# The first mixer in another order, and norms whose sums are begun early

## The chip, the cores and the metric

One core of one Trainium2 chip runs the kernel. The metric is device time in microseconds of one execution, median over several. Five engines work in parallel and meet at semaphores: TensorE (PE; its weight loads are shown as PEld), VectorE (DVE), ScalarE (ACT), GpSimd (POOL), and SyncE (SP), which here only issues DMAs.

## The reference

Two stacks of two layers each follow one another on x of 256 tokens by 1024, all in float32. The change touches the input and mixer of the first layer and nearly all norms.

```
def hybrid_mixer(x, ...):                  # first layer
    xr, yr, q, k, v, iq, ik, iw = split(x @ w_in, [512, 512, 512, 64, 64, 256, 64, 4])
    xr = causal_depthwise_conv(xr, conv_w, conv_b)            # 4 taps
    rec = rg_lru(xr, ...) * gelu(yr)                          # linear recurrence over time
    att = dsa_attention(q, k, v, iq, ik, iw)                  # 8 heads of 64
    return concatenate([rec, att]) @ w_out
def rg_lru(x, ...):
    r, i = sigmoid(x @ w_a + b_a), sigmoid(x @ w_x + b_x)     # blocks of 64
    a = exp(-8 * r * softplus(-lam)); u = sqrt(1 - a * a) * (i * x)
    h[t] = a[t] * h[t-1] + u[t]
def dsa_attention(q, k, v, iq, ik, iw):
    isc = sum over h of relu(iq[h] @ ik) * iw[h]              # index scores, causal
    keep the 64 highest isc of each row; logits = q @ k * scale - slope * distance
    return softmax(logits over the kept ones) @ v
def first_block(x):
    for i in (0, 1):
        m = hybrid_mixer(x) if i == 0 else mla_mixer(x)
        h = layer_norm(ALPHA * x + m, ln1)
        f = square(relu(h @ w1)) @ w2; e = sigmoid(h @ w_gate) * (p @ w_proj)
        x = layer_norm(ALPHA * h + f + e, ln2)
def layer_norm(x): mu = mean(x); return (x - mu) * rsqrt(mean((x - mu)**2) + 1e-5) * g + b
def rms_norm(x):   return x * rsqrt(mean(x * x) + 1e-6) * g
```

The second stack has two layers, each with an RMS norm, dense projections with three token mixers (retention, a delta-rule recurrence, a short convolution), and 32 experts; a last RMS norm ends it.

## The kernel before

Features lie on the 128 partitions, tokens along the free dimension: a tile of xT, hT, R or SQ is 128 features by 256 tokens, eight of them make the width. A product "pair" is two output tiles of 256 tokens, each the sum of K products (8 for a width of 1024), in one of four PSUM banks; a product of float32 shows as two records. `bank_full` and `bank_read` count fills and evictions of each bank, which go round in the order of `BANK_USES`. Every engine has its instructions in an order written out by hand, and waits in it; SP issues weight blocks of 2 MB into the ring slots 0 to 3 as their last reader releases them.

First mixer. SP issues the constant table (4,179 columns, the identity first), the vectors, x, the gate blocks, two small column blocks for V, and w_in in blocks of 512 columns into slots 0 and 1. TensorE waits for constants and x, turns x into xT (L756), and runs eight pairs (`hy_in`: xr, yr, q, then K, index queries and index K; the 64 K columns and the 64 index-K columns stand twice in their block, put there by two DMAs each, so that both halves of the partitions get them). DVE and ACT evict them in turn. Then V with the index weights (`dsa_v`, 68 columns, 16 products), the index dots (`idx`), the gates (`rg_gates`, which wait for GpSimd's `conv_done`) and the attention. DVE makes the index scores (L1571, L1574), takes the top 64 by 8 rounds of MAX8 and MATCH_REPLACE8, and makes the mask (to L1593). GpSimd does the convolution (L2611 to L2616), the cubic part of gelu (L2624 to L2626), and parts of the decay (L2632 to L2637). In the attention, DVE's `masked_max` of a pair of heads (L1635 to L1647) and the four parts of the recurrence stand in one program: `recurrence(0)` is the reciprocal of L1603, parts 1 and 2 hold products and the scans (L1606 to L1618), part 3 the last product. GpSimd scales the probabilities (L2644), TensorE turns them (L823), ACT evicts (L2352), and TensorE makes the output. `hy_out` is four pairs, each evicted by DVE into R with ALPHA * x added (L1667).

Layer norm (`layer_norm` of each engine): TensorE sums the eight tiles of R over the partitions with a matrix of ones, so that each partition has the sum; DVE makes the mean (L1512) and takes it off R two tiles at a time (L1516); ACT squares (L2296); TensorE sums the squares; DVE makes variance plus epsilon (L1504), ACT the root (L2284), DVE the reciprocal (L1506) and scales tile by tile (L1520); ACT puts gain and bias on (L2289), and the next product starts on a tile when it is there (`ready`). `clear_acc` zeroes the accumulators of the feed-forward behind it. RMS norm: the same from the squares on, without a mean. Five RMS norms are here: two in the second layer's attention (of query and K/V), one ahead of each layer of the second stack, one at the end.

Of the kernel before, what the change touches and what calls it, by code (L numbers as in the profile page):

```python
# [19 lines left out]
P = 128  # L20
D = 1024
# [149 lines left out]
BANK_USES = [("x_in", 4), ("hy_in", 8), ("dsa_v", 1), ("idx", 4), ("rg_gates", 4), ("dsa", 4 * 2), ("hy_out", 4)]  # L171
# [96 lines left out]
def build(nc, a, out):  # L268

    with ExitStack() as ctx:  # L270
# [51 lines left out]
        def bcast(ap, n):  # L322
# [5 lines left out]
            "inputs_loaded", "x_loaded", "p_loaded", "small_loaded", "kvw_loaded", "tail_loaded", "pos_loaded",  # L328
            "lam_abs", "lam_log", "lam_ready", "conv_done", "decay_in", "decay_tanh", "decay_den", "decay_sqrt", "gelu_in", "gelu_sig", "rec_done",
            "dsa_max", "dsa_exp", "dsa_sum", "dsa_probs", "probs_turned", "probs_read", "att_full", "att_read",  # L330
            "norm_in", "norm_sum", "norm_centered", "norm_sq", "norm_var", "norm_std", "norm_scaled", "norm_out",
# [30 lines left out]
        VI = GT[:, 12:13, :]  # L362
        MIX = YB[:, 0:8, :]
# [6 lines left out]
        FF = PR[:, 32:40, :]  # L370

# [47 lines left out]
        def vi(tt, c0, c1):  # L419
            return flat(VI)[:, tt * 68 + c0:tt * 68 + c1]  # L420


        @block.sync
        def _(sp):
# [50 lines left out]
            def lin8(name, w):  # L475
# [3 lines left out]
            sp.dma_start(const[:], a["const"]).then_inc(sems["inputs_loaded"], 16)  # L479
            sp.dma_start(vec[:], a["vectors"]).then_inc(sems["inputs_loaded"], 16)  # L480
            sp.dma_start(R[:].rearrange("p (t k) s -> p t (k s)", t=TT), a["x"][0].rearrange("(t p) d -> p t d", p=P)).then_inc(sems["x_loaded"], 16)

            sp.dma_start(small_w[:], a["gate_blocks"]).then_inc(sems["small_loaded"], 16)
            w_in = a["hy_w_in"][0]
            tail = w_in[:, 1536:1988].rearrange("(k p) n -> p k n", p=P)
            sp.dma_start(GT[:, 20:24, :].rearrange("p a b -> p (a b)")[:, 0:KT * 68].rearrange("p (k n) -> p k n", k=KT)[:, :, 0:64],
                         tail[:, :, 64:128]).then_inc(sems["kvw_loaded"], 16)
            sp.dma_start(GT[:, 20:24, :].rearrange("p a b -> p (a b)")[:, 0:KT * 68].rearrange("p (k n) -> p k n", k=KT)[:, :, 64:68],
                         tail[:, :, 448:452]).then_inc(sems["kvw_loaded"], 16)


            s0, s1 = 0, 1
            r0 = ring[0][:].rearrange("p (k n) -> p k n", k=KT)
            r1 = ring[1][:].rearrange("p (k n) -> p k n", k=KT)
            sp.dma_start(r0, w_in[:, 0:512].rearrange("(k p) n -> p k n", p=P)).then_inc(slot_full[0], 16)
            sp.dma_start(r1, w_in[:, 512:1024].rearrange("(k p) n -> p k n", p=P)).then_inc(slot_full[1], 16)
            n0 = BANK_AT["hy_in"]
            sp.wait_ge(bank_full[(n0 + 1) % BANKS], filled(n0 + 1))
            sp.dma_start(r0, w_in[:, 1024:1536].rearrange("(k p) n -> p k n", p=P)).then_inc(slot_full[0], 16)
            sp.wait_ge(bank_full[(n0 + 3) % BANKS], filled(n0 + 3))  # L500
            for c, (c0, c1) in ((0, (0, 64)), (64, (0, 64)), (128, (128, 384)), (384, (384, 448)), (448, (384, 448))):

                sp.dma_start(r1[:, :, c:c + c1 - c0], tail[:, :, c0:c1]).then_inc(
                    slot_full[1] if c == 448 else sems["tail_loaded"], 16)
            released[0] = (bank_full[(n0 + 5) % BANKS], (n0 + 5) // BANKS + 1)
            released[1] = (bank_full[(n0 + 7) % BANKS], (n0 + 7) // BANKS + 1)
# [163 lines left out]
        def _(pe):  # L670
# [42 lines left out]
            def sums(src, K, piece, first=0):  # L713

                for i in range(K):
                    k = (first + i) % K
                    if k % 2 == 0:
                        piece(k // 2)
                    ins = mul(acc[3][:, 0:S], C("ones"), src[:, k, :], i == 0, i == K - 1)
                ins.then_inc(sems["norm_sum"], 1)  # L720

            def squared(q):
                pe.wait_ge(sems["norm_sq"], L.nxt("norm_sq"))

            def layer_norm(piece):
                sums(R, KT, piece)
                sums(SQ, KT, squared)
                L.nxt("norm_var")

            def rms_norm(src=SQ, K=KT, first=0):  # L730
                sums(src, K, squared, first)
                L.nxt("norm_var")
# [16 lines left out]
            pe.wait_ge(sems["inputs_loaded"], 32)  # L749
            pe.wait_ge(sems["x_loaded"], L.nxt("x_loaded", 16))  # L750
# [12 lines left out]
            n0 = BANK_AT["hy_in"]  # L763
            for b in range(4):
                pe.wait_ge(slot_full[b % 2], loaded(b // 2))
                if b == 3:
                    pe.wait_ge(sems["tail_loaded"], L.nxt("tail_loaded", 64))
                W = slot(b % 2, KT)
                for j in range(2):
                    pair(n0 + 2 * b + j, lambda h, k: W[:, k, (2 * j + h) * P:(2 * j + h + 1) * P],  # L770
                         lambda k: xT[:, k, :], KT)
# [4 lines left out]
            for tt in range(TT):  # L776
                for k in range(KT):
                    ins = mul(bk(n)[:, tt * 68:(tt + 1) * 68], xT[:, k, tt * P:(tt + 1) * P], kvw[:, k, :],
                              k == 0, k == KT - 1)
# [1929 lines left out]
```

## Time and profile before

| | |
|---|---|
| median of 3 runs (lowest, highest) | 2717.18 us (2714.19, 2719.2) |
| the profiled execution, its span | 2715.58 us, 2713.7 us |
| mean granted TensorE clock of that execution | 0.922 of full |
| TensorE busy | 2266.8 us (84%) |
| DVE, ACT, GpSimd busy | 681.5 us, 375.7 us, 60.6 us |
| moved by DMA | 655.01 MB, mean 241 GB/s |

The profiler takes one execution, with the start and length of each instruction and what released it. Times count from the start of the span. A timeline row merges neighbours of one kind: its second number is the time from the first start to the last end, the count stands at its end, and in brackets is the engine's idle time ahead with what ended it. The granted clock is 1.00 at 2.4 GHz and 0.50 at 1.2 GHz. A busy engine is not at its peak, and an idle one costs nothing unless it is waited for.

### The profile page before, as it was taken

The numbers are of one execution on the slowest core, as the hardware profiler recorded it, in microseconds if no ns is written. First come the engines' busy times: TensorE is split into PE (matmuls) and PEld (weight loads), VectorE is DVE, ScalarE is ACT, GpSimd is POOL, SyncE is SP. The second block draws the span as 40 slices with busy tenths as digits, with TensorE's granted clock in tenths as the row PEclk, the third lists the DMA queues.
The fourth block names the chain that finished last, engine by engine and source line by source line (L and its number), as shares of the span: only waits on it lengthen the run. The fifth ranks groups of instructions, "written<-read, shape, count | busy, mean of one in ns | idle before, by whom it ended". The sixth has DMA issues, their size and how long they took to land.

```text
span 2713.7 us, 28029 instructions
## 1 busy us (share of the span) xinstructions
PE 2266.8 (84%) x12294; PEld 1634.7 (60%) x12294; DVE 681.5 (25%) x1233; ACT 375.7 (14%) x730; POOL 60.6 (2%) x69
## 2 busy tenths in 40 slices
PE   7599999989999899999966656569999997666665
PEld 6478887668888688998622222238898873222222
DVE  0723212433220454432210000015343221000002
ACT  0310011141000321011100000013111110000001
POOL 3200000010000000000000000000000000000000
PEclk9789999999999899999998888889999998778777
DMA  6047642208762333124899999963322389999996
GB/s 225 27 176 312 271 185 95 97 1 325 271 267 81 102 109 127 63 94 180 349 409 409 409 409 409 409 245 127 124 78 94 125 346 409 409 409 409 409 409 248
DMA packets 202986, 655.01 MB, mean 241 GB/s; under 512 B 15736, under 2 KB 20600, under 8 KB 198392
## 3 DMA queue, kind: packets, MB, share of 16 engines
q1 hardware_dynamic: 202872, 653.32, 62.4%
q8 instruction: 92, 1.51, 0.2%
q14 instruction: 22, 0.18, 0.0%
HBM read 652.25 MB, written 1.05 MB: 241 GB/s over the span
## 4 chain that ended last, share of the span: by engine, by line
PE 64%; DMA 28%; DVE 4%; ACT 2%; issue 1%; SPq 0%; POOL 0%; DVEq 0%; ACTq 0%
PE bank L676 63%; DMA PRGT<-in_w_exp_gate 8%; DMA PRGT<-in_w_exp_up 7%; DMA ring<-in_w_exp_up 6%; DMA ring<-in_w_exp_gate 3%; DMA PRGT<-in_w_exp_down 3%; DMA ring<-in_w_exp_down 1%; DVE stat L1506 1%; PE bank L1056 0%; DMA ring<-in_hy_w_in 0%; DVE sm L1644 0%; POOL PRGT L2644 0%; ACT R L2561 0%; DVE PRGT L1587 0%; DVE R L1603 0%
## 5 line engine op out<-in xcount | busy, mean ns | idle before, releaser
L676 PE MATMUL bank<-hT,ring 128*128 128x256 f32 x3392 | 755.8, 383 | 10.1 <-ACT hT L2289 10.1
L676 PEld LDWEIGHTS bank<-hT,ring 128*128 128x128 f32 x3392 | 645.5, 192 | 105.2 <-issue 17.2
L676 PE MATMUL bank<-PRGT,ring 128*128 128x256 f32 (+4 forms) x1936 | 415.0, 377 | 3.3 <-ACT PRGT L2289 2.2
L676 PEld LDWEIGHTS bank<-PRGT,ring 128*128 128x128 f32 (+3 forms) x1936 | 353.0, 187 | 61.8 <-issue 5.5
L676 PE MATMUL bank<-PRGT,R 128*32 128x512 f32 x1120 | 170.4, 741 | 107.5 <-DMA PRGT<-in_w_exp_up 69.2
L676 PE MATMUL bank<-ring,R 128*32 128x512 f32 (+1 forms) x960 | 157.7, 769 | 111.5 <-DMA ring<-in_w_exp_up 56.7
L676 PEld LDWEIGHTS bank<-PRGT,R 128*32 128x32 f32 x1120 | 35.5, 123 | 233.0 <-DMA PRGT<-in_w_exp_up 110.6
L676 PE MATMUL bank<-PRGT,SQ 128*32 128x512 f32 (+1 forms) x768 | 110.9, 654 | 72.4 <-DMA PRGT<-in_w_exp_down 61.3
L676 PEld LDWEIGHTS bank<-ring,R 128*32 128x32 f32 (+1 forms) x960 | 34.9, 130 | 226.5 <-DMA ring<-in_w_exp_up 93.1
L1685 DVE SCALAR_TENSOR_TENSOR PRGT<-PRGT,sm 128x3072 f32<-128x3072 f32 x28 | 95.7, 3419 | 233.8 <-DMA PRGT<-in_w_ada 233.7
L676 PEld LDWEIGHTS bank<-PRGT,SQ 128*32 128x32 f32 (+1 forms) x768 | 34.7, 133 | 135.6 <-DMA PRGT<-in_w_exp_down 83.9
L676 PE MATMUL bank<-xT,ring 128*128 128x256 f32 (+1 forms) x368 | 84.2, 393 | 9.5 <-DMA ring<-in_hy_w_in 5.5
L676 PE MATMUL bank<-ring,SQ 128*32 128x512 f32 (+1 forms) x448 | 59.3, 612 | 30.8 <-DMA ring<-in_w_exp_down 22.5
L2228 DVE TENSOR_TENSOR SQ<-SQ,bank 128x512 f32<-128x512 f32 x16 | 11.0, 688 | 294.1 <-ACT SQ L2570 294.1
L676 PEld LDWEIGHTS bank<-xT,ring 128*128 128x128 f32 (+1 forms) x368 | 71.2, 195 | 22.4 <-issue 10.6
L2231 DVE TENSOR_TENSOR SQ<-SQ,bank 128x512 f32<-128x512 f32 x16 | 11.0, 688 | 275.9 <-PE bank L676 275.9
L676 PEld LDWEIGHTS bank<-SQ,hT 128*128 128x128 f32 x512 | 63.4, 205 | 18.2 <-issue 18.2
L2376 ACT ACTIVATE PRGT<-bank 128x512 f32<-128x512 f32 x32 | 19.1, 597 | 373.0 <-PE bank L676 373.0
L676 PE MATMUL bank<-PRGT 128*128 128x128 f32 (+4 forms) x400 | 52.3, 306 | 20.8 <-DVE PRGT L1635 15.5
L2240 DVE COPY R<-bank 128x512 f32<-128x512 f32 x16 | 11.1, 692 | 231.9 <-PE bank L676 231.9
L2561 ACT ACTIVATE R<-bank,sm 128x128 f32<-128x128 f32 x64 | 24.1, 457 | 318.7 <-PE bank L676 318.7
L2426 ACT ACTIVATE PRGT<-bank 128x512 f32<-128x512 f32 x42 | 25.1, 597 | 305.6 <-PE bank L676 305.6
(324 smaller groups left out, 1871.3 us busy)
## 6 DMA issues: line engine op xcount, KB each, us to landing
PRGT<-in_w_exp_down SPq DMA_DIRECT2D x40, 2048.0 KB, 24.0
PRGT<-in_w_exp_gate SPq DMA_DIRECT2D x36, 2048.0 KB, 23.8
PRGT<-in_w_exp_up SPq DMA_DIRECT2D x34, 2048.0 KB, 24.3
ring<-in_mlp_w SPq DMA_DIRECT2D x32, 2048.0 KB, 7.7
ring<-in_w_exp_up SPq DMA_DIRECT2D x30, 2048.0 KB, 24.2
ring<-in_w_exp_gate SPq DMA_DIRECT2D x28, 2048.0 KB, 24.1
PRGT<-in_w_ada SPq DMA_DIRECT2D x32, 1536.0 KB, 10.6
ring<-in_w_exp_down SPq DMA_DIRECT2D x24, 2048.0 KB, 23.9
```

The costliest lines, as they stand in the source:

```text
L676: return mm(o, lhsT=lhsT, rhs=rhs, start=first, stop=last, **kw)
L1506: v.reciprocal(stat[:, 1, :], stat[:, 1, :]).then_inc(sems["vec_chain"], 1)
L1685: v.scalar_tensor_tensor(total, ADA[h], sm[:, bass.ds(k, 1)], total, ALU.mult, ALU.add).then_inc(sems["ada_summed"], 1)
L2228: v.tensor_tensor(SG, SG, bank[0][:, :], ALU.mult).then_inc(sems["vec_chain"], 1)
L2231: v.tensor_tensor(SG, SG, bank[1][:, :], ALU.mult).then_inc(sems["gu_read"], 1)
L2240: v.tensor_copy(YE[:, 0:512], bank[2][:, :]).then_inc(sems["y_read_v"], 1)
L2376: f(tile_, bk(n)[:, :], ACT.Relu).then_inc(bank_read[n % BANKS], 1)
L2426: f(flat(PR[:, in_tiles(p), :]), acc[b][:, :], ACT.Copy).then_inc(dense_read[b], 1)
L2561: ins = f(XS[:, k * P:(k + 1) * P], bank[3][:, (k - 4) * P:(k - 3) * P], ACT.Identity, bias=sm[:, SPERM + k:SPERM + k + 1], scale=sm[:, GP ...
```

## The change

First mixer. Only the identity's columns go ahead of x. The block w_in[:, 1536:1988] (K, V, index queries, index K, index weights) is loaded first, whole, by one DMA; K and index K are doubled by TensorE, which multiplies the same 64 columns into both halves of the output. V's two column groups are separate products now. The order of products is K and index (`hy_kv`), V, index dots, xr, the first yr pair, gates, the second yr pair, q, attention. The convolution's taps are made by ACT, and GpSimd only adds them; ACT has the decay's scaling and its denominator, the tanh with a scale, and all evictions but one. `recurrence(0)` stands ahead of the first `masked_max`, and the other parts stay behind their pairs of heads.

Norms. The variance is made as the mean of squares minus the squared mean, so squares are taken of R itself. In layer norm 1 GpSimd adds the pairs 0, 1 and 2 of R and of the squares, while the output product runs, and TensorE sums only those two tiles and pair 3. In layer norm 2 TensorE sums R and squares alternately, all 16 tiles. DVE scales each tile by the reciprocal root and takes mean times reciprocal root off it one tile behind. RMS norms: ACT takes the root right from the sum, with scale and epsilon; the last three have GpSimd add three pairs of squares. `gains(0)` moves behind the second layer's attention.

```diff
-BANK_USES = [("x_in", 4), ("hy_in", 8), ("dsa_v", 1), ("idx", 4), ("rg_gates", 4), ("dsa", 4 * 2), ("hy_out", 4)]
+BANK_USES = [("x_in", 4), ("hy_kv", 2), ("dsa_v", 1), ("idx", 4), ("hy_xr", 2), ("hy_yr0", 1), ("rg_gates", 4),
+             ("hy_yr1", 1), ("hy_q", 2), ("dsa", 4 * 2), ("hy_out", 4)]
...
+            sp.dma_start(const[:, 0:P], a["const"][:, 0:P]).then_inc(sems["x_loaded"], 16)
+            sp.dma_start(R[:].rearrange("p (t k) s -> p t (k s)", t=TT), a["x"][0].rearrange("(t p) d -> p t d", p=P)).then_inc(sems["x_loaded"], 16)
+            sp.dma_start(*hy_block(0, 1536, 1988)).then_inc(slot_full[0], 16)
             sp.dma_start(vec[:], a["vectors"]).then_inc(sems["inputs_loaded"], 16)
+            sp.dma_start(const[:, P:], a["const"][:, P:]).then_inc(sems["inputs_loaded"], 16)
+            sp.dma_start(*hy_block(1, 0, 512)).then_inc(slot_full[1], 16)
             sp.dma_start(small_w[:], a["gate_blocks"]).then_inc(sems["small_loaded"], 16)
...
+            def norm_of_output(m):
+                sq = L.nxt("norm_sq", 4) - 4
+                pe.wait_ge(sems["presummed"], L.nxt("presummed"))
+                add_up(TOTAL, tiles_of(RSUM, 0), True, False)
+                add_up(TOTAL2, tiles_of(SQ, 0), True, False)
+                pe.wait_ge(bank_read[m % BANKS], filled(m))
+                add_up(TOTAL, tiles_of(R, 3), False, True).then_inc(sems["norm_sum"], 1)
+                pe.wait_ge(sems["norm_sq"], sq + 4)
+                add_up(TOTAL2, tiles_of(SQ, 3), False, True).then_inc(sems["norm_sum"], 1)
+                L.nxt("norm_var")
...
+            def rms_norm_presummed(first, last):
+                sq = L.nxt("norm_sq", 4) - 4
+                pe.wait_ge(sems["presummed"], L.nxt("presummed"))
+                add_up(TOTAL, tiles_of(SQ, first), True, False)
+                pe.wait_ge(sems["norm_sq"], sq + 4)
+                add_up(TOTAL, tiles_of(SQ, last), False, True).then_inc(sems["norm_sum"], 1)
...
+            for j, (c_twice, c_once) in enumerate(((0, 128), (384, 256))):
+                n = n0 + j
+                pe.wait_ge(bank_read[n % BANKS], emptied(n))
+                o = bk(n)
+                for k in range(KT):
+                    for half in (slice(0, 64), slice(64, 128)):
+                        mul(o[half, j * S:(j + 1) * S], W[:, k, c_twice:c_twice + 64], xT[:, k, :], k == 0, k == KT - 1)
+                for k in range(KT):
+                    ins = mul(o[:, (1 - j) * S:(2 - j) * S], W[:, k, c_once:c_once + P], xT[:, k, :], k == 0, k == KT - 1)
+                ins.then_inc(bank_full[n % BANKS], 1)
...
+            pe.wait_ge(slot_full[1], loaded(0))
+            for j in range(2):
+                hy_pair(BANK_AT["hy_xr"] + j, slot(1, KT), 2 * j)
+            pe.wait_ge(slot_full[0], loaded(1))
+            hy_pair(BANK_AT["hy_yr0"], slot(0, KT), 0)
             pe.wait_ge(sems["small_loaded"], L.nxt("small_loaded", 16))
             pe.wait_ge(sems["conv_done"], L.nxt("conv_done"))
...
+            hy_pair(BANK_AT["hy_yr1"], slot(0, KT), 2)
...
-                for q in range(4):
-                    r_ = R[:, 2 * q:2 * q + 2, :]
-                    v.tensor_tensor(r_, r_, bcast(stat[:, 0, :], 2), ALU.subtract).then_inc(sems["norm_centered"], 1)
...
+                v.tensor_scalar(var, var, 0.0, 1e-5, ALU.max, ALU.add).then_inc(sems["norm_var"], 1)
+                inverse()
+                v.tensor_tensor(mean, mean, var, ALU.mult).then_inc(sems["vec_chain"], 1)
+                c0 = L.nxt("norm_centered", KT) - KT
+                v.tensor_tensor(R[:, 0, :], R[:, 0, :], var, ALU.mult).then_inc(sems["norm_centered"], 1)
+                dve.wait_ge(sems["vec_chain"], L.up())
                 for k in range(KT):
+                    if k + 1 < KT:
+                        v.tensor_tensor(R[:, k + 1, :], R[:, k + 1, :], var, ALU.mult).then_inc(sems["norm_centered"], 1)
+                    dve.wait_ge(sems["norm_centered"], c0 + k + 1)
+                    v.tensor_tensor(R[:, k, :], R[:, k, :], mean, ALU.subtract).then_inc(sems["norm_scaled"], 1)
...
+                if slopes:
+                    recurrence(0)
                 masked_max(0)
...
+                    if slopes and hp:
                         recurrence(hp)
...
+                f(stat[:, 1, :], acc[3][:, 0:S], ACT.Sqrt, bias=C("eps"), scale=1.0 / width).then_inc(sems["norm_std"], 1)
...
+                for c in (2 * j, 2 * j + 1):
+                    f(PR[:, XC + c, :], PR[:, XR + c, :], ACT.Identity, bias=V_("conv_b")[:, c:c + 1], scale=V_("conv_w3")[:, c:c + 1])
+                    for i in range(3):
+                        sh = 3 - i
+                        ins = f(TAP[i][:, c, sh:S], PR[:, XR + c, 0:S - sh], ACT.Copy, scale=V_(f"conv_w{i}")[:, c:c + 1])
+                    ins.then_inc(sems["conv_taps"], 1)
...
+                pool.wait_ge(sems["conv_taps"], c + 1)
                 for i in (2, 1, 0):
                     sh = 3 - i
+                    ins = g.tensor_tensor(dst[:, sh:S], dst[:, sh:S], TAP[i][:, c, sh:S], ALU.add)
...
+            def presum(a_, b_, c_):
+                sq = L.nxt("norm_sq", 4) - 4
+                pool.wait_ge(sems["norm_sq"], sq + 2)
+                chained(nc.gpsimd.tensor_tensor(both(a_), both(a_), both(b_), ALU.add))
+                pool.wait_ge(sems["norm_sq"], sq + 3)
+                nc.gpsimd.tensor_tensor(both(a_), both(a_), both(c_), ALU.add).then_inc(sems["presummed"], 1)
```

## Rows read from the trace of the kernel before

**Rows 1.** Page, part 4: the chain that ended last, by engine.

```profile
PE 64%; DMA 28%; DVE 4%; ACT 2%; issue 1%; SPq 0%; POOL 0%; DVEq 0%; ACTq 0%
```

**Rows 2.** Timeline, start: start us, us, engine, line, operation, tiles, count.

```profile
12.51 3.65 PE L756 MATMUL bank<-const,R 128*128 128x128 f32 x16 [12.51 <-DMA R<-in_x]
...
21.65 57.93 PE L676 MATMUL bank<-xT,ring 128*128 128x256 f32 x256 [5.49 <-DMA ring<-in_hy_w_in]
```

**Rows 3.** Windows: busy of PE, PEld, DVE, ACT, POOL; PE clock, DMA share, GB/s.

```profile
8.00:10.00 2.00, 0.00 (x0) 0.00 (x0) 0.00 (x0) 0.00 (x0) 0.00 (x0) 1.00 1.00 404
24.00:26.00 2.00, 2.00 (x6) 1.61 (x5) 0.00 (x0) 0.00 (x0) 0.00 (x0) 0.50 0.91 335
```

**Rows 4.** Timeline of the first mixer, until its attention begins.

```profile
42.52 0.72 POOL L2616 TENSOR_TENSOR PRGT<-PRGT,R 128x254 f32<-128x254 f32 x1
...
79.41 3.68 PE L676 MATMUL bank<-PRGT,xT 128*128 128x68 f32 x32
...
83.03 1.68 PE L676 MATMUL bank<-PRGT 64*128 64x128 f32 x16
...
84.64 3.72 PE L676 MATMUL bank<-PRGT,small_w 128*128 128x256 f32 x16
...
85.76 0.29 DVE L1571 TENSOR_SCALAR PRGT<-PRGT,sm 128x128 f32<-128x128 f32 x1 [1.91 <-ACT PRGT L2316]
...
93.75 2.35 POOL L2635 TENSOR_TENSOR PRGT<-PRGT 128x1024 f32<-128x1024 f32 x1
...
105.38 0.55 DVE L1635 SCALAR_TENSOR_TENSOR PRGT<-const,bank 128x384 f32<-128x384 f32 x1
```

**Rows 5.** Timeline of the first attention and its output product.

```profile
112.69 6.52 DVE L1603 RECIPROCAL R<-R 128x1024 f32<-128x1024 f32 x1
...
112.85 1.61 POOL L2644 TENSOR_TENSOR PRGT<-PRGT,sm 128x256 f32<-128x256 f32 x2 [14.01 <-DVE sm L1652]
...
123.10 3.48 POOL L2644 TENSOR_TENSOR PRGT<-PRGT,sm 128x256 f32<-128x256 f32 x2 [8.64 <-DVE sm L1652]
...
142.82 27.89 PE L676 MATMUL bank<-PRGT,ring 128*128 128x256 f32 x128 [0.47 <-ACT PRGT L2356]
```

**Rows 6.** Timeline of the same; groups of TensorE by shape (busy us, mean ns).

```profile
117.58 1.43 PE L676 MATMUL bank<-SQ,PRGT 128*64 128x256 f32 x8
...
L676 PE MATMUL bank<-ring 128*64 128x64 f32 x64 | 2.4, 226 | 0.0
```

**Rows 7.** Timeline of layer norm 1, first layer.

```profile
170.99 3.62 PE L676 MATMUL bank<-R,const 128*128 128x256 f32 x16
...
176.62 5.41 PE L676 MATMUL bank<-SQ,const 128*128 128x256 f32 x16 [2.01 <-ACT SQ L2296]
...
183.04 1.75 DVE L1506 RECIPROCAL stat<-stat 128x256 f32<-128x256 f32 x1 [0.48 <-ACT stat L2284]
...
184.83 2.77 DVE L1520 TENSOR_TENSOR R<-R,stat 128x256 f32<-128x256 f32 x8
...
186.04 15.80 PE L676 MATMUL bank<-hT,ring 128*128 128x256 f32 x64 [0.38 <-ACT hT L2289]
```

**Rows 8.** Timeline of layer norm 2, first layer.

```profile
447.62 3.62 PE L676 MATMUL bank<-R,const 128*128 128x256 f32 x16
...
462.56 26.28 PE L676 MATMUL bank<-xT,ring 128*128 128x256 f32 x112 [4.01 <-ACT xT L2289]
```

**Rows 9.** Timeline of later norms: two in the middle, the last one.

```profile
909.89 1.75 DVE L1506 RECIPROCAL stat<-stat 128x256 f32<-128x256 f32 x1 [0.48 <-ACT stat L2284]
...
915.26 2.50 DVE L1820 TENSOR_TENSOR SQ<-xT 128x512 f32<-128x512 f32 x4
...
916.00 6.11 PE L676 MATMUL bank<-SQ,const 128*128 128x256 f32 x16 [7.13 <-DVE SQ L1820]
...
1806.69 6.21 PE L676 MATMUL bank<-SQ,const 128*128 128x256 f32 x16 [4.18 <-ACT SQ L2296]
...
2695.83 4.25 PE L676 MATMUL bank<-SQ,const 128*128 128x256 f32 x16 [1.76 <-ACT SQ L2296]
```

More of the change, by code:

```diff
@@ L485, in _ @@
[L485 to L489, printed above, removed]
@@ L500, in _ @@
[L500 to L506, printed above, removed]
+            n = BANK_AT["dsa_v"]
@@ L507, in _ @@
+            sp.wait_ge(bank_full[n % BANKS], filled(n))
+            sp.dma_start(*hy_block(0, 512, 1024)).then_inc(slot_full[0], 16)
+            n = BANK_AT["hy_xr"] + 1
+            sp.wait_ge(bank_full[n % BANKS], filled(n))
+            sp.dma_start(*hy_block(1, 1024, 1536)).then_inc(slot_full[1], 16)
+            for s, n in ((0, BANK_AT["hy_yr1"]), (1, BANK_AT["hy_q"] + 1)):
+                released[s] = (bank_full[n % BANKS], filled(n))
             lin8("hy_out", a["hy_w_out"][0])
@@ L730, in rms_norm, with add_up, tiles_of @@
-            def rms_norm(src=SQ, K=KT, first=0):
-                sums(src, K, squared, first)
-                L.nxt("norm_var")
+            def add_up(o, tiles, first, last):
+                for i, t in enumerate(tiles):
+                    ins = mul(o, C("ones"), t, first and i == 0, last and i == len(tiles) - 1, skip_group_check=True)
+                return ins
+            TOTAL, TOTAL2 = acc[3][:, 0:S], acc[2][:, 0:S]
+            def tiles_of(src, *pairs):
+                return [src[:, 2 * q + h, :] for q in pairs for h in range(2)]
@@ L780, in _ @@
+                    ins = mul(o[:, 64:68], xT[:, k, tt * P:(tt + 1) * P], W[:, k, 448:452], False, tt == TT - 1 and k == KT - 1,
+                              skip_group_check=True)
             ins.then_inc(bank_full[n % BANKS], 1)
-            for m in range(BANK_AT["hy_in"] + 4, BANK_AT["hy_in"] + 8):
+            for m in (n0, n0 + 1):
                 pe.wait_ge(bank_read[m % BANKS], filled(m))
@@ L803, in _ @@
                     ins.then_inc(bank_full[n % BANKS], 1)
+            hy_pair(BANK_AT["hy_yr1"], slot(0, KT), 2)
+            pe.wait_ge(slot_full[1], loaded(1))
+            for j in range(2):
+                hy_pair(BANK_AT["hy_q"] + j, slot(1, KT), 2 * j)
+            for m in (BANK_AT["hy_q"], BANK_AT["hy_q"] + 1):
+                pe.wait_ge(bank_read[m % BANKS], filled(m))
             def attention(name, pairs, done, q, k, v):
```

301 lines of the change are left out of this document (160 added, 141 removed).

## The prediction

> **What bounds the kernel now.** I read the page's chain first: TensorE holds 64% of it and DMA 28% [rows 1]. The DMA part lies in the expert stages, whose loads are released by semaphores of the stage before, so whatever is saved ahead of them moves them whole. The change touches no expert stage; I therefore read only the first mixer and the nine normalisations, in the timeline, and ask at each place what ends the wait.
>
> First mixer. TensorE waits for x until 12.51 us, transposes it, and waits again, for the first weights, until 21.65 [rows 2]. It then runs 256 records of products, the V product, the index dots and the gates back to back until about 88.4 [rows 2, 4]. But the attention starts only at 105.38: DVE gets its first index score at 85.76 and needs 19.6 us for scores, top-64 and mask [rows 4]. That is the first exposed piece. The second lies in the attention: DVE works without a gap, and in it stands a 6.52 us reciprocal of the recurrence [rows 5]. The output product begins at 142.82.
>
> Normalisations. Layer norm 1 sums R on TensorE (3.62 us), lets DVE subtract the mean, squares, sums again (5.41 us, with a gap of 2 us ahead), then goes through variance, square root and reciprocal; TensorE gets its first tile at 186.04, 15.05 us after the first sum began [rows 7]. Layer norm 2 takes 14.94 [rows 8].
>
> **The change, part by part.** All times below are of the profiled execution (2715.58 us; its span is 2713.7). The median of the runs shown is 2717.18, 1.6 higher, and the forecast is carried over to it at the end.
>
> *Start.* x now queues behind 64 KB of the identity instead of the whole constant table and the vectors (2,089.5 and 201 KB). 2.28 MB at the 404 GB/s of [rows 3] is 5.6 us, so x lands at 12.4 - 5.6 = 6.8 (TensorE starts on it at 12.51 now). Transposes 6.9 to 10.5, last copy 11.2. The first weight block (8 x 128 rows of 452 columns, 1.85 MB) follows directly: 4.6 us, 11.4. Products start at 11.4 instead of 21.65. If the two interleaved neighbours (vectors, rest of the table) slow it, 13 to 15.
>
> *TensorE's work until the attention.* Before: 57.93 + 3.68 + 1.68 + 3.72 [rows 2, 4]. The 57.93 contain a beginning at the lower of the two clock levels (0.50, 1.2 GHz [rows 3]): at the rate of the output product, 27.89 for 128 [rows 5], 256 records are 55.8, so 2.1 were lost. The pause ahead shrinks from 5.5 us to about 1; I take half the loss, 57.0. The K and index-K columns, which were doubled by five small DMAs, are now doubled on TensorE: 16 more products of 64 columns. Do the halves run side by side? The row for 64-column products that alternate between halves says yes: 64 records in 2.4 us, 38 ns each, against the 115 ns of the V product's 68-column records with all 128 columns of weights [rows 4, 6]. The attention's output product says rather no: 1.43 us for 8 records of 768 streamed columns in two passes, which at 27.89/128 per 256 is 1.31 without any overlap [rows 6]; but there each half issues two in a row. I take overlap, 0 us; the other end is 16 x 2 x 0.218 = 7.0. The Trainium skill (TensorEngine Tiling (Array Packing), Key Properties) says that different tiles can load weights and multiply in parallel; by it the sum stands as it is, by the second row it would be 7.0 longer; this trace has a row on either side. The V product becomes 64 records (64 columns, then 4) instead of 32. At 68 columns one took 3.68/32 = 0.115 us, twice what its columns stream in, so I take it as the price of its weights and not of its columns: 64 x 0.115 = 7.4, +3.7; if the 4-column ones went by their columns, about +0.2. Sum: 57.0 + 7.4 + 1.7 + 3.7 = 69.8.
>
> *The gates' wait.* TensorE now stands in order at conv_done between hy_yr0 and the gates, with hy_yr1 and hy_q behind it. The last two taps come from ACT about 4 us after hy_xr's second pair; GpSimd needs 3 additions each, 0.72 [rows 4] + 0.1, so 2.5 us for a channel tile and conv_done is some 7.3 after that pair; hy_yr0 covers 7.0. Stall 0.5. If each addition costs what a GpSimd row costs beside DVE work with two inputs (3.48 against 1.61 [rows 5]), 12 additions take 19.9 and the stall is 8.
>
> *Index chain.* It starts at 11.4 + 1.2 + 13.9 + 7.4 + 1.7 + 1 = 36.6 and ends near 56.5, when TensorE has over 25 us of products left: hidden entirely. Without that cover it would cost its 19.6. Later slot loads are released 7 us or more before they are needed, as now. Next late is TensorE itself: 11.4 + 69.8 + 0.5 = 81.7, then 1.2 for the eviction of hy_q and the first logits. Attention at 82.9 instead of 105.38: **-22.5**.
>
> *Attention.* The gates are done near 61 and their denominator on ACT near 65, so the reciprocal runs at 65 to 72 under the products. DVE's sequence loses 6.52 [rows 5]: **-6.5**. The other parts stay where they were.
>
> *Layer norm 1, twice.* GpSimd adds the first three pairs (R and squares) during the output product, whose pairs are 6.9 us apart; a 512-wide addition is about 1.3 (between 0.72 for 254 and 2.35 for 1024 [rows 4]). TensorE then needs 8 products, 3.62: from 170.99 to 174.61, instead of two sums to 182.03. To the reciprocal it was 1.01 (183.04 - 182.03); one DVE operation more, 0.35 (2.77/8): 175.97; reciprocal 1.75: 177.72 [rows 7]. From its end to TensorE's first tile it was 1.25; mean times rstd, the next scaling and the subtraction stand ahead of it now, 3 x 0.35: 180.0. So 6.0 less each, **-12.0**. The tiles now come every 0.70 instead of 0.35 on DVE; while the clock is low a product takes 0.87 and this costs nothing; at the full clock up to 8 x 0.27 = 2 each.
>
> *Layer norm 2, first layer.* Squares are ready early, so 16 products run through from 447.62: 7.1 instead of about the 11.0 of layer norm 1; + 0.35 + 1.05: **-2.5** [rows 7, 8].
>
> *RMS norms.* ACT takes the root straight from the sum: half of that 1.01, **-0.5**, at the query norm (the K/V one is covered). In the second norm chain of the last first-block layer, layer norm 2 gains 3.5 at its reciprocal, but DVE's 17 operations of 0.35 push its squares to 6.4 us after it instead of 3.6 (915.26 - 911.64) and GpSimd's two additions (2.6) follow; then 4 products instead of 8, which ran mostly at the low clock (6.11 [rows 9]): 3.5 + 2.6 + 0.5 - 2.8 - 2.8 = **-1.0**; if GpSimd waits for DVE's squares, +1. Between the layers (6.21 for 8 products after the last square but one [rows 9]) half the products go, less the wait for an addition: **-2.1**. At the end the sums were paced by the squares and closed 1.2 after the last (4.25 [rows 9]); now GpSimd's second addition ends 0.6 after it and 4 products at the low clock take 3.5: +2.4 - 0.5 = **+1.9**, +0.4 at the full clock. The moved gains() runs under the 28 us of mla_out, where DVE waits.
>
> Sum: -22.5 - 6.5 - 12.0 - 2.5 - 0.5 - 1.0 - 2.1 + 1.9 = **-45.2**; 2670.4 in a profiled execution, 2672 as a median.
>
> **Rivals.**
> *A. GpSimd holds TensorE.* The convolution's additions and the early sums meet DVE's two-input operations. For: 3.48 against 1.61. Against: during the index chain DVE mostly runs one-input operations, and the 1024-wide GpSimd product there took 2.35 [rows 4]. +8 at the gates, +2 at the norms: 2682. Beside it the Trainium skill (SBUF — State Buffer, SBUF: two separate sides) calls the port that DVE and GpSimd share an exclusive lock for the whole instruction; by this rule only operations with two SBUF inputs or a two-port mode block, and the pair 3.48 and 1.61 agrees, the latter beside a reciprocal.
> *B. The halves take turns,* +7.0: 2679.
> *C. The tiles' pace decides in the norms.* At the full clock 2 each in four norms: +8 at most, 2676 to 2680.
> *D. No change:* the expert stages are DMA-bound and could absorb the gain, if their loads were not released by it. Against: TensorE waits for loads issued after merged and chunk_used. 2717.
> *E. Slower.* TensorE stays at the 1.2 GHz level through the mixer. Its 69 us of products would take 67 more: 2672 + 67 = 2739; it turns slower once 45 us of full-rate work run at half. Against: 57.93 for 256 records, with 55.8 at the full rate, leaves room for no more than the first few at half.
>
> **How the numbers follow.** Forecast 60%, A 12%, B 8%, C 12%, D 3%, E 2%, and 3% for a larger gain (start or clock better by over 7). The forecast's own range: start -1 to +3, clock 1.2 either way, gates 0 to 3, norms -2 to +3: 2666 to 2678. With A, B and C up to 2683; low end 2664. 0.2% is 5.4 us, about what a measurement of this kernel tells from no change. Faster 0.95, same 0.03, slower 0.02.
>
> **What would show it.** In the profile after: products starting near 11.4; the index score near 37 and its mask near 57 under running products; an idle stretch of TensorE at the gates (under 1 us right, 5 or more A); the two hy_kv banks taking about 14 us together (21 if B holds); attention at 83; output product at 113.8; first tile 9.0 us after layer norm 1's first sum. The forecast is wrong if the attention starts after 90, or if a norm gains under 4 us.

## The result, and the profile after

| | before | after |
|---|---|---|
| median (lowest, highest), same chip | 2716.03 us (2714.19, 2719.2), 4 runs | 2680.69 us (2677.28, 2684.91), 4 runs |
| ratio, 95% interval | | 0.9869 (0.9852 to 0.9887) |
| profiled execution, span | 2715.58 us, 2713.7 us | 2679.7 us, 2677.9 us |

The kernel is 35.3 us faster; the forecast was 45.2 us less. The spans differ by 35.8, so 9.4 of the predicted us are missing. I cut the span at seven starts that both traces show, into eight pieces. Each runs from one start to the next.

| until | before | after | change | predicted |
|---|---|---|---|---|
| first masked maximum | 105.38 | 87.21 | -18.2 | -22.5 |
| output product of the mixer | 37.44 | 31.08 | -6.4 | -6.5 |
| first tile behind layer norm 1 | 43.22 | 38.99 | -4.2 | -6.0 |
| first tile behind layer norm 2 | 276.52 | 275.01 | -1.5 | -2.5 |
| first tile behind the second layer norm 1 | 173.80 | 166.74 | -7.1 | -6.5 |
| first tile of the dense stage | 289.75 | 290.19 | +0.4 | -1.0 |
| last product of the last expert stage | 1764.27 | 1762.52 | -1.8 | -2.1 |
| end | 23.32 | 26.16 | +2.8 | +1.9 |

The chain that ended last, by engine, in the page after; it answers to [rows 1]:

```profile
PE 64%; DMA 29%; DVE 3%; ACT 1%; SPq 1%; POOL 1%; issue 1%; POOLq 0%; DVEq 0%; ACTq 0%
```

TensorE's timeline of the kernel after, from the first products to the output product (start us, us, engine, line, operation, tiles, count):

```profile
11.37 14.58 PE L671 MATMUL bank<-xT,ring 128*64 128x256 f32 x96 [1.65 <-DMA ring<-in_hy_w_in]
25.78 10.03 PE L671 MATMUL bank<-ring,xT 128*128 128x64 f32 x64
35.74 3.09 PE L671 MATMUL bank<-PRGT 64*128 64x128 f32 x16
38.77 21.58 PE L671 MATMUL bank<-xT,ring 128*128 128x256 f32 x96
61.06 3.69 PE L671 MATMUL bank<-PRGT,small_w 128*128 128x256 f32 x16 [0.72 <-issue]
64.59 20.88 PE L671 MATMUL bank<-xT,ring 128*128 128x256 f32 x96
86.21 2.53 PE L671 MATMUL bank<-PRGT 64*128 64x128 f32 x20 [0.73 <-issue]
...
118.29 29.66 PE L671 MATMUL bank<-PRGT,ring 128*128 128x256 f32 x128 [0.47 <-ACT PRGT L2435]
```

And DVE's beside it: the first index score, the end of the mask, the reciprocal of the recurrence, the first masked maximum.

```profile
39.71 0.29 DVE L1612 TENSOR_SCALAR PRGT<-PRGT,sm 128x128 f32<-128x128 f32 x1 [2.75 <-ACT PRGT L2367]
...
59.62 0.76 DVE L1634 TENSOR_SCALAR PRGT<-PRGT 128x384 f32<-128x384 f32 x1
...
68.41 6.55 DVE L1653 RECIPROCAL R<-R 128x1024 f32<-128x1024 f32 x1 [7.16 <-ACT R L2405]
...
87.21 0.55 DVE L1686 SCALAR_TENSOR_TENSOR PRGT<-const,bank 128x384 f32<-128x384 f32 x1 [12.25 <-PE bank L671]
```

Products start at 11.37 (before 21.65 [rows 2]; forecast 11.4). Index chain and reciprocal both end under running products, and DVE then waits 12.25 us for TensorE: the exposed 19.6 us of [rows 4] are gone. TensorE's two short waits are marked "issue", but the rows of the engines that it waits for by the program end 0.10 us before it starts: GpSimd's last additions of the convolution at 59.25 + 1.71 = 60.96, ahead of the gates at 61.06, and ScalarE's eviction of q at 86.11, ahead of the logits at 86.21.

```profile
59.25 1.71 POOL L2690 TENSOR_TENSOR PRGT<-PRGT,SQ 128x254 f32<-128x254 f32 x2
...
85.51 0.60 ACT L2333 ACTIVATE PRGT<-bank 128x512 f32<-128x512 f32 x1 [6.31 <-PE bank L671]
```

From xr's first product to the first masked maximum it is 87.21 - 38.77 = 48.44 us, where the forecast had 57.0 - 13.9 + 3.7 + 0.5 + 1.2 = 48.5. What is off stands before it: V and the index dots hold TensorE for 38.77 - 25.78 = 12.99 us where the sum had 7.4 + 1.7 = 9.1. The windows of that stretch say why (busy of PE, PEld, DVE, ACT, GpSimd; granted clock; DMA share; GB/s):

```profile
27.00:29.00 2.00, 2.00 (x21) 2.00 (x19) 0.00 (x0) 0.00 (x0) 0.00 (x0) 1.00 0.00 0
29.00:31.00 2.00, 2.00 (x14) 2.00 (x14) 0.00 (x0) 0.00 (x0) 0.00 (x0) 0.69 0.00 0
31.00:33.00 2.00, 2.00 (x12) 2.00 (x11) 0.00 (x0) 0.00 (x0) 0.00 (x0) 0.50 0.00 0
...
37.00:39.00 2.00, 2.00 (x11) 1.26 (x10) 0.00 (x0) 1.17 (x3) 0.00 (x0) 0.50 0.91 233
39.00:41.00 2.00, 2.00 (x8) 1.69 (x9) 1.18 (x4) 0.58 (x2) 0.00 (x0) 0.75 1.05 410
41.00:43.00 2.00, 2.00 (x11) 1.77 (x10) 1.86 (x5) 0.00 (x0) 0.00 (x0) 1.00 1.02 383
```

TensorE is shown busy without a gap here, and yet the granted clock falls to 0.50 (1.2 GHz) from about 30 to 40: 21 records in 2 us become 12. The same level stands at the output product's start (0.50 in 118 to 120, 0.52 in 120 to 122, then 1.00), which takes 29.66 us instead of the 27.89 of [rows 5].

Layer norm 1 of the kernel after: the sums, the reciprocal, the first tile.

```profile
148.23 1.03 PE L671 MATMUL bank<-PRGT,const 128*128 128x256 f32 x4
...
149.10 1.03 PE L671 MATMUL bank<-SQ,const 128*128 128x256 f32 x4
...
153.28 1.75 DVE L1549 RECIPROCAL stat<-stat 128x256 f32<-128x256 f32 x1 [0.48 <-ACT stat L2359]
...
157.28 1.19 PE L671 MATMUL bank<-hT,ring 128*128 128x256 f32 x2 [1.80 <-ACT hT L2340]
```

From first sum to first tile it is 9.05 us, 6.00 less than the 15.05 of [rows 7], as forecast. The two rows of four records each (two products) are the sums over the pair of tiles into which GpSimd has added three pairs, of R and of the squares. The next rows are of the three RMS norms that GpSimd serves in the kernel after (ahead of the dense stage, between the layers, the last): DVE's squares, GpSimd's additions, TensorE's sums; they answer to [rows 9].

```profile
876.83 2.49 DVE L1873 TENSOR_TENSOR SQ<-xT 128x512 f32<-128x512 f32 x4
878.20 2.25 POOL L2738 TENSOR_TENSOR SQ<-SQ 128x512 f32<-128x512 f32 x1 [292.03 <-DVE SQ L1873]
880.52 1.26 POOL L2740 TENSOR_TENSOR SQ<-SQ 128x512 f32<-128x512 f32 x1
881.84 3.78 PE L671 MATMUL bank<-SQ,const 128*128 128x256 f32 x8 [13.84 <-POOL SQ L2740]
...
1767.86 1.27 POOL L2738 TENSOR_TENSOR SQ<-SQ 128x512 f32<-128x512 f32 x1 [812.01 <-ACT SQ L2353]
...
2655.47 4.12 DVE L2312 SCALAR_TENSOR_TENSOR xT<-bank,mod,xT 128x256 f32<-128x256 f32 x8 [3.83 <-PE bank L671]
...
2658.26 1.27 POOL L2738 TENSOR_TENSOR SQ<-SQ 128x512 f32<-128x512 f32 x1 [811.99 <-ACT SQ L2353]
...
2659.60 1.26 POOL L2740 TENSOR_TENSOR SQ<-SQ 128x512 f32<-128x512 f32 x1
...
2660.92 3.78 PE L671 MATMUL bank<-SQ,const 128*128 128x256 f32 x8 [5.49 <-POOL SQ L2740]
...
2665.31 1.75 DVE L1549 RECIPROCAL stat<-stat 128x256 f32<-128x256 f32 x1 [5.72 <-ACT stat L2345]
```

The same 512-wide addition takes 2.25 us where DVE's squares run beside it, with both inputs in SBUF. It takes 1.27 beside L2312 of DVE, which reads one of its two tensors from a PSUM bank (2658.26; L2312 runs to 2659.59), and 1.26 with DVE idle (2659.60). At the end TensorE waits for the second addition, then sums in 3.78 us, where before the sums ran along with the squares [rows 9].

### The profile page after: what moved, and what is told of

It reads as the page before. It is cut to its first block, busy times and chain, and to the rows that moved or that the text cites. A ratio compares the mean times of both kernels' runs of the same rounds, so it can differ in the third digit from the quotient of the medians.

```text
span 2677.9 us, 28088 instructions
## 1 busy us (share of the span) xinstructions
PE 2240.8 (84%) x12302; PEld 1620.2 (61%) x12302; DVE 685.2 (26%) x1253; ACT 390.5 (15%) x754; POOL 59.7 (2%) x62
## 4 chain that ended last, share of the span: by engine, by line
PE 64%; DMA 29%; DVE 3%; ACT 1%; SPq 1%; POOL 1%; issue 1%; POOLq 0%; DVEq 0%; ACTq 0%
PE bank L671 64%; DMA PRGT<-in_w_exp_gate 7%; DMA ring<-in_w_exp_up 7%; DMA PRGT<-in_w_exp_up 5%; DMA PRGT<-in_w_exp_down 4%; DMA ring<-in_w_exp_gate 3%; DMA ring<-in_w_exp_down 2%; SPq L617 1%; DVE stat L1549 1%; PE bank L1101 1%; DMA ring<-in_hy_w_in 0%; DVE sm L1695 0%; POOL PRGT L2713 0%; PE bank L867 0%; ACT R L2641 0%
## 5 line engine op out<-in xcount | busy, mean ns | idle before, releaser
L671 PE MATMUL bank<-hT,ring 128*128 128x256 f32 x3392 | 757.3, 383 | 11.4 <-ACT hT L2340 11.4
L671 PE MATMUL bank<-xT,ring 128*128 128x256 f32 (+2 forms) x400 | 83.4, 388 | 7.0 <-ACT xT L2340 5.3
L671 PEld LDWEIGHTS bank<-xT,ring 128*128 128x128 f32 (+2 forms) x400 | 68.7, 183 | 21.5 <-issue 9.7
L671 PE MATMUL bank<-SQ,hT 128*128 128x128 f32 x512 | 65.0, 288 | 0.0
```

Of the source, the lines that this page charges most:

```text
L671: return mm(o, lhsT=lhsT, rhs=rhs, start=first, stop=last, **kw)
```

## The experiments

Each edit is against the kernel after. A kernel with one execution has its profile alone; the others have a median and a ratio to the kernel before, taken on the same chip.

| kernel | us | ratio (95%) |
|---|---|---|
| wide V products | 2673.69, one | |
| V and index weights in one product | 2670.67, 4 runs (2669.62 to 2674.84) | 0.9842 (0.9826 to 0.9859) |
| K halves one after the other | 2682.39, one | |
| last sum without GpSimd | 2674.55, one | |
| mixer's part alone | 2692.50, 4 runs (2689.36 to 2697.61) | 0.9914 (0.9897 to 0.9930) |
| norms' part alone | 2707.14, 7 runs (2702.56 to 2708.68) | 0.9967 (0.9956 to 0.9978) |
| squares on ScalarE | 2683.12, one | |
| recurrence back inside | 2686.21, one | |
| V in one + last sum without GpSimd | 2669.04, 5 runs (2667.18 to 2673.09) | 0.9835 (0.9822 to 0.9849) |
| the same + squares on ScalarE | 2669.82, 5 runs (2669.51 to 2674.98) | 0.9838 (0.9825 to 0.9852) |

**Does the shape of the V products bring the clock down?** The 4-column product of all k but the last gets 64 columns, of which 60 are read by nobody; the count of records stays.

```diff
+                    if k < KT - 1:
+                        mul(o[:, 64:128], xT[:, k, tt * P:(tt + 1) * P], ring[0][:, k * 452 + 448:k * 452 + 512], False, False,
+                            skip_group_check=True)
+                        continue
                     ins = mul(o[:, 64:68], xT[:, k, tt * P:(tt + 1) * P], W[:, k, 448:452], False, tt == TT - 1 and k == KT - 1,
```

> The changed kernel, but 14 of the 16 four-column products behind V stream 64 columns (the four and sixty of the neighbouring weights, whose sums nobody reads). Number of records stays 64. Theory (the V stage lost because its records carry so few columns that the granted clock fell to half, which then also slowed the index dots and the start of the xr products): V takes about 7.4 us instead of 10.0, the dots 1.7 to 2.2 instead of 3.0, the clock stays at 1.00, the attention starts about 4.5 us earlier than 87.2. Rival (the number of records alone sets the 10.0 us, or the clock would have fallen there anyway): V stays at 10.0 or grows, no change of the attention's start.

TensorE's timeline, and two windows over the stretch:

```profile
25.89 7.21 PE L671 MATMUL bank<-ring,xT 128*128 128x64 f32 x64
33.02 1.68 PE L671 MATMUL bank<-PRGT 64*128 64x128 f32 x16
```

```profile
25.00:29.00 4.00, 4.00 (x34) 3.87 (x32) 0.00 (x0) 0.60 (x1) 0.00 (x0) 1.00 0.00 0
29.00:33.00 4.00, 4.00 (x38) 4.00 (x36) 0.00 (x0) 0.00 (x0) 0.00 (x0) 1.00 0.00 0
```

The short products have sixteen times the columns, the records are as many, and the stage is 2.8 us shorter: the clock stays at 1.00. V and index dots take 34.64 - 25.89 = 8.75 us, against the forecast's 9.1, and the first masked maximum comes at 82.49, 4.7 us earlier (the theory had 4.5). So the forecast's price of a record was right (7.21/64 = 0.113 us at the full level); what it lacked was the clock.

**One product instead of two.** Both column groups lie 384 apart, and one product takes 64 columns of each (128 streamed, 68 used).

```diff
+                    if k < KT - 1:
+                        w_ = ring[0][:, k * 452 + 64:k * 452 + 832].rearrange("p (b c) -> p b c", b=2)[:, :, 0:64]
+                        mul(two(o), x_, w_, tt == 0 and k == 0, False, skip_group_check=True)
+                        continue
```

> The changed kernel with V and index weights as one product of 128 columns in two blocks (68 of them used) for 7 of 8 pieces, so 36 records instead of 64. Theory (64 records at the price of their weights, and the clock lost besides): V takes 4.2 us, the dots 1.7 to 2.0, the attention starts 7 to 8 us earlier than 87.2; the time falls by 7 to 8, to about 2673, a ratio to the kernel before of 0.984. Rival (only the number of records counts, without the clock): 4.4 earlier, about 2676. Rival 2 (TensorE's end is not what starts the attention): no change.

The masked maximum starts at 79.33, 7.9 us earlier than in the kernel after, as the theory had it. The median is 10.0 us lower; by the ratios, each to the kernel before run beside it, it is 7.3. The V row:

```profile
25.84 4.08 PE L671 MATMUL bank<-ring,xT 128*128 128x128 f32 x36
```

36 records in 4.08 us are again 0.113 each, and 28 of them stream 128 columns: up to 128 the columns cost nothing here.

**Do the halves of K run side by side?** The loops over k and over the halves change places.

```diff
-                for k in range(KT):
-                    for half in (slice(0, 64), slice(64, 128)):
+                for half in (slice(0, 64), slice(64, 128)):
+                    for k in range(KT):
```

> The changed kernel, but the doubled K and index-K products run all eight pieces of one half and then all eight of the other, instead of alternating. Theory (two 64-column products run side by side only if neighbours in the queue go to different halves): each of the two doubled blocks takes 6.9 us instead of 3.6, so hy_kv takes 21 us instead of 14.4, and the attention starts about 6.6 later. Rival (64-column products cost half as much for another reason, fewer weights to load): no change.

```profile
11.20 21.80 PE L671 MATMUL bank<-xT,ring 128*64 128x256 f32 x96 [1.37 <-DMA ring<-in_hy_w_in]
```

21.80 us instead of 14.58, both at clock 1.00. The 7.2 us are the 7.0 that my sum gave for no overlap. So both rows of [rows 6] are right: neighbours in different halves overlap, two in a row in one half do not. The masked maximum starts at 92.68, 5.5 later; in this execution the V stage gave 2.1 back (7.95 us for 10.03), since the clock fell later in it.

**The last norm's sum in the old way,** from four pairs of squares, each as it comes.

```diff
-            rms_norm_presummed(3, 2)
+            for q in (3, 0, 1, 2):
+                pe.wait_ge(sems["norm_sq"], L.nxt("norm_sq"))
+                ins = add_up(TOTAL, tiles_of(SQ, q), q == 3, q == 2)
+            ins.then_inc(sems["norm_sum"], 1)
...
-            presum(3, 0, 1)
```

> The changed kernel, but the last norm sums its squares on TensorE pair by pair as they come (8 products), without GpSimd. Theory (the sums were paced by the squares before, and GpSimd's chain ends later than they did): from the last expert product's end of accumulation to the end 22.9 us, which is 0.5 less than before and 3.3 less than the 26.2 of the changed kernel. Rival (the longer end comes from the clock or the output's DMA): it stays at 26.

Rows of this kernel:

```profile
2649.72 3.69 PE L671 MATMUL bank<-stat,R 128*128 128x256 f32 x16 [0.86 <-DVE R L2297]
...
2655.17 4.24 PE L671 MATMUL bank<-SQ,const 128*128 128x256 f32 x16 [1.76 <-ACT SQ L2356]
...
2660.11 1.75 DVE L1552 RECIPROCAL stat<-stat 128x256 f32<-128x256 f32 x1 [2.55 <-ACT stat L2348]
```

From the last product to the end it is 2672.7 - 2649.72 = 22.98 us, against 26.16 after and 23.32 before. The reciprocal starts 10.39 us after the start of the last product (2660.11 - 2649.72), and in the kernel after 13.57 (2665.31 - 2651.74, the start of its last product). The early sum costs 3.2 us at this place.

**Each part alone.** One kernel has the mixer's part with the norms as before, the other the norms' part with the mixer as before. Their cores, first the mixer's part alone, then the norms':

```diff
-                norm_of_output(BANK_AT[mixer] + 3)
+                layer_norm(lambda q: pe.wait_ge(bank_read[(m0 + q) % BANKS], filled(m0 + q)))
...
-                norm_of_sum()
+                layer_norm(lambda q: pe.wait_ge(sems["norm_in"], L.nxt("norm_in")))
...
-                rms_norm_presummed(3 * l, 3 - l)
+                rms_norm(first=6 if l else 0)
```

```diff
-            for j, (c_twice, c_once) in enumerate(((0, 128), (384, 256))):
...
+            n0 = BANK_AT["hy_in"]
+            for b in range(4):
...
+                for j in range(2):
+                    pair(n0 + 2 * b + j, lambda h, k: W[:, k, (2 * j + h) * P:(2 * j + h + 1) * P],
+                         lambda k: xT[:, k, :], KT)
```

> The mixer's part of the change alone (start, order of the stages, recurrence beside the products), with the normalisations as before. Theory (the parts add, and the mixer's part is everything up to the sum of hy_out): products start at 11.4 us instead of 21.65, the granted clock falls in the V stage as in the whole change (V about 10, index columns about 3.1 us), hy_out's product starts near 118.3 instead of 142.8 us, and of these 24.5 us hy_out's low clock takes 1.8 back: 22.7 us less, about 2693 us. Rival (the norms' part needs the mixer's or the other way round, so that they don't add): away from that by over 2 us, above all if hy_out's 1.8 us or a later stage's pace turns out to hang on the norms.

> The normalisations' part alone, with the first mixer as before. Theory: LN1 of both layers 6.0 us each shorter, LN2 of the first layer 2.6, the RMS norm between the layers 1.6, the one between the norms of the middle 0.1 longer, the last norm 2.8 longer; the tile pace after a norm and the stages behind it give back 1 to 2: 12 us less, about 2703 to 2705 us; the stage between LN1's first tile and LN2 of the first layer is then 1.2 us longer here too. Rival (that 1.2 us belongs to the mixer, by the clock or the loads it moved): it is 261.6 here as before, and the total about 2702.

By the medians, against the 2714.82 of the kernel before beside them, the mixer's part gives 22.3 us and the norms' part 7.7, together 30.0; by the ratios 23.3 (19.0 to 28.0) and 9.0 (6.0 to 11.9), together 32.3, against 35.6 (30.7 to 40.2) for the whole. They add within what the intervals leave. The mixer's forecast of 2693 was hit; the norms' median is 2 to 4 us above its 2703 to 2705, and why is open. Its profiled execution (2703.48, the second fastest of seven) shows the steps as forecast: 6.0 less for layer norm 1, 2.5 less for layer norm 2. The disputed 1 us of the feed-forward stage did not come with the norms alone: from layer norm 1's first tile to layer norm 2's sums it is 261.58 us, as in the kernel before. In a longer measure, from ScalarE's first tile behind layer norm 1 to that behind layer norm 2 it is 276.53 us before, 278.05 with the mixer's part, 274.00 with the norms' part, 275.02 with both, and 274.05 to 274.98 in the eight others of the kernels here, which have the same code in it as the kernel after. So the same code loses anything from nothing to 1 us there. The windows behind the norm show the clock as a difference; that it is the cause was not tested: 0.50 for the first 5 us in the kernel after (first row), 0.64 with the norms' part alone (second).

```profile
157.00:162.00 5.00, 4.72 (x11) 3.84 (x12) 3.86 (x12) 4.58 (x9) 0.00 (x0) 0.50 1.03 400
```

```profile
180.00:185.00 5.00, 4.88 (x15) 4.03 (x16) 3.70 (x12) 4.57 (x8) 0.00 (x0) 0.64 1.03 397
```

**The first half of the recurrence back inside the attention.**

```diff
-                if slopes:
-                    recurrence(0)
                 masked_max(0)
...
-                    if slopes and hp:
+                    if slopes:
```

> The whole change, but the first half of the recurrence stands back inside the attention, behind the first masked maximum, as in the kernel before. Theory (DVE is the engine whose work fills the attention, and 6.4 us of it were moved beside the products): from the first masked maximum to hy_out's product 37.4 us instead of 31.1, total 6.3 us more than the whole change, about 2687 us. Rival (the attention is shorter because something else in it moved): 31 to 33 us, total within 2 us of the whole change.

From the masked maximum at 89.03 to the output product at 126.48 it is 37.45 us, as in the kernel before (37.44), and 31.08 after. The reciprocal stands at 96.35 with 6.52 us. That step is shown. The total of this one execution is 5.5 us above the median of the kernel after, near the theory's 6.3.

**Squares on ScalarE in the norm ahead of the dense stage.**

```diff
-                        v.tensor_tensor(flat(SQ[:, 2 * q:2 * q + 2, :]), x_, x_, ALU.mult).then_inc(sems["norm_sq"], 1)
+                    dve.wait_ge(sems["norm_out"], L.nxt("norm_out", 8))
...
+            def square_pair(q):
+                act.wait_ge(sems["norm_out"], 30 + 2 * (q + 1))
+                f(flat(SQ[:, 2 * q:2 * q + 2, :]), flat(xT[:, 2 * q:2 * q + 2, :]), ACT.Square).then_inc(sems["norm_sq"], 1)
```

> The whole change, but the squares of the RMS norm between LN2 of the first layer and the dense stage are made by ScalarE, pair by pair between its own tiles, instead of by DVE. Theory (GpSimd's addition of two 512-wide tiles takes 2.26 us there because DVE's square runs beside it, and 1.27 where nothing does): the addition takes about 1.3 us, the sum starts a microsecond earlier, and ScalarE's squares, some 0.55 us each, delay its last tile by up to 1.6 us of which the early sum gives back part: from LN2's sums to the dense stage's first tile 27 to 28 us instead of 28.3. Rival (the 2.26 us is the addition's own, by its operands or its place): it stays above 2 us, and the stretch is as long or a microsecond longer.

```profile
876.62 1.40 POOL L2743 TENSOR_TENSOR SQ<-SQ 128x512 f32<-128x512 f32 x1 [290.46 <-ACT SQ L2334]
...
878.19 1.27 POOL L2745 TENSOR_TENSOR SQ<-SQ 128x512 f32<-128x512 f32 x1 [0.17 <-ACT SQ L2334]
...
886.94 3.42 PE L671 MATMUL bank<-hT,ring 128*128 128x256 f32 x8 [3.70 <-ACT hT L2343]
...
1762.34 6.05 PE L671 MATMUL bank<-stat,R 128*128 128x256 f32 x16 [0.86 <-DVE R L2291]
```

The additions take 1.40 and 1.27 us, so the 2.25 was not the addition's own. From layer norm 2's sums to the dense stage's first tile it is 26.0 us (886.94 - 860.91) where the theory had 27 to 28 and the kernel after has 28.3. Of these 2.3 us, 1.6 are the earlier start of the additions (876.62 against 878.20), because ScalarE's squares are ready sooner. The span is all the same 3.4 us longer than that of the kernel after. One execution does not show that the kernel is slower: the four of the kernel after lie between 2677.28 and 2684.91. But it shows where this one lost its lead, in the expert stage. The stream of weights is ahead by only 0.74 at its end (issue of the next stage's block at 1739.83 against 1740.57), and then the last product of the stage takes 6.05 us, mostly at clock 0.50. In the kernel after it takes 3.69 at 1.00.

**Two costs taken away together, without and with ScalarE's squares.**

> Whole change with two of its costs taken away: value and index columns in one matrix product per pair of tiles (68 columns at once, all but the last tile), and the last normalisation's sum taken over all four pairs of tiles without GpSimd's additions. Theory (the two add, since they stand 2600 us apart): 8 to 10 us and 3 to 4 us less than the whole change, about 2668 us, ratio to the kernel before 0.983. Rival (the granted clock in the expert stages takes a part back, as it varies there with where a stage begins): 2670 to 2675.

> The same with ScalarE's squares in the RMS norm before the first dense stage. Theory (the 2.3 us saved there reach the end): 2.3 us less than with DVE's squares, about 2666 us. Rival (the expert stage behind it goes by the weights' transfer, whose stream was ahead by only 0.7 us at its end in the run with ScalarE's squares, and by the granted clock of its last products): the same within 1 us as with DVE's squares, though the norm is 2.3 us shorter.

Without: 2669.04 us, 11.7 less than the kernel after (9.2 by the ratios), near the theory's 2668. With: 2669.82, where the theory had 2.3 less. That agrees with the rival but does not decide: the two sets of five runs overlap (2667.18 to 2673.09, 2669.51 to 2674.98), and each ratio is known to 3.7 us either way. The traces show in one execution each what the rival says. The weights' stream is 2.06 us ahead at the start of the stage (issue at 1276.26 against 1278.32) and 0.4 at 1301; then the stage's last product takes 6.09 against 3.69 us. The 6.05 and the 6.09 are from two kernels; whether they come with ScalarE's squares or by chance of the clock stays open.

## Why the prediction was right or wrong

The time is 8.7 us above the forecast. It is above the 2666 to 2678 that I gave the forecast itself, and below the 2683 that the rivals A, B and C were to reach. None of these came as I had put it, so that the wide range holds the time is in part luck: its room was made for other causes.

- *Start, index chain, attention:* right. 11.37 against 11.4; chain hidden; 6.4 against 6.5 us, and the experiment with the recurrence shows what it hangs on.
- *Overlap of the halves:* right, shown. Rival B has its 7.2 us only where each half is a run of its own.
- *Gates' wait:* 0.72 against 0.5, behind GpSimd's last addition as forecast. Rival A's +8 did not come.
- *From xr on:* 48.44 against 48.5, in part by luck. The 57.0 kept half of the loss at the start, 1.2 us, but the clock is at 1.00 from the first products on (10 to 14 us). In its place came 0.6 of low clock in xr's products behind the index dots (21.58 us, and 20.99 in the kernel with wide V products) and 0.5 more between the last product and the first masked maximum (1.7 for 1.2).
- **V product and index dots, 7.4 + 1.7:** the term that failed. The price per record was right, the clock was taken as full for the whole mixer but its start. Measured 12.99 at mostly the lower level, 3.9 more. With K's 0.5 more, that is 4.4 us, of which 0.1 came back. I had looked for the lower level at the pause ahead of the products ("I take half the loss") and, in rival E, in the whole mixer or nowhere; it came in the middle, from the short products that the change itself makes.
- *Output product:* taken as unchanged; it began at 0.50, +1.8. This is not a fixed cost of the change: with the same code there it took 27.89 us in the kernel with the last sum without GpSimd, where the clock was back at 1.00 by 118 us, and 28.48 to 29.60 in the eight others.
- *Layer norm 1, twice; layer norm 2:* 6.0 and 2.5 as forecast. The feed-forward behind the first gave 1.0 back and behind the second 0.3 (262.60 and 261.89 us to the next sums, against 261.58); rival C had 2 each at the full clock, and the windows behind the first show the lower level instead.
- **Norm ahead of the dense stage, -1.0:** +0.4. My text had the case ("if GpSimd waits for DVE's squares, +1") and chose the other. The addition took 2.25 instead of 1.3, because DVE's squares ran beside it, as the kernel with ScalarE's squares shows; 0.3 of the other 0.4 lie in the second feed-forward. The sum's terms here are gains, and it takes 2.8 for additions that its text puts at 2.6.
- **Last norm, +1.9:** mechanism right, size +2.8, shown: the old way of summing ends 3.2 us sooner. Of the 0.9 that the forecast is short, 0.5 is arithmetic: its own figures, 0.6 + 3.5 - 1.2 - 0.5, come to 2.4. The sum then took 3.78 instead of 3.5.

By the table, in its order: 4.3 + 0.1 + 1.8 + 1.0 - 0.6 + 1.4 + 0.4 + 0.9 = 9.3, the missing 9.4 but for rounding.

## What to carry to other kernels

Short products cost by the record: here 0.113 us up to 128 columns. Splitting one in two doubles it, and in the kernels here the clock fell in a stretch of very short ones, for itself and for what followed. An early sum on a third engine pays where the main work still runs and costs where the last square ends the chain (3 us). What it pays was not run alone: layer norm 1 gained 6.0 us with it and with squares that don't wait for the mean, layer norm 2 gained 2.5 with the second alone, which leaves an estimated 3.5 for the early sum. Time saved ahead of a stage that goes by its transfers may not arrive: judge it at the end, over several runs.

## What the runs showed of the hardware that I had not expected

- The granted clock fell to 0.50 with TensorE busy without a gap, in all six profiled kernels that have the 4-column products throughout (V stage 7.95 to 10.17 us, index dots 3.09), and in none of the four that keep them for the last tile of features alone (index dots 1.68 or 1.69). The Trainium skill (TensorE: Matmul & The Clock Gate, Part 1: The HAM clock gate) ties the lower level to an idle TensorE and the higher to a busy one. The trace agrees on the two levels; that an engine shown as busy can lose the higher one is the measurement's word.
- The products of the block with K and the index columns, in alternating halves, took 14.58 us in five profiles and 16.48 to 16.75 in four (mixer alone, recurrence inside, and the two last kernels), at clock 1.00 in both groups, with identical code. They differ in the first products alone: 12 records in 12 to 14 us instead of 22. What decides it stays open; it is worth 2 us of these totals.
- GpSimd's addition of 512 columns: 1.26 us with DVE idle, 1.27 beside DVE's L2312 with one input in PSUM, 2.25 from 878.20 on, when the last of DVE's squares still ran to 876.83 + 2.49 = 879.32. From their end it has 1.13 left, nearly all of its length: it hardly moved beside them. The Trainium skill (SBUF — State Buffer, SBUF: two separate sides) has a port that GpSimd and a DVE operation with two SBUF inputs hold in turn, each for its whole instruction; the trace agrees, with 2.25 against 1.27 beside an operation that has one SBUF input.
